# Two-layer transformer trunk on one core: the hidden product of both MLPs with weight blocks as stationary operand and 256 tokens as moving one

## What is computed

```python
def sq_relu_mlp(h, w1, w2):          # w1: (2048, 8192), w2: (8192, 2048)
    return jnp.square(jax.nn.relu(h @ w1)) @ w2

h = modulate(rms_norm(x, norm_g[layer, 1]), shift_m, scale_m)
x = x + gate_m[:, None, :] * sq_relu_mlp(h, mlp_w1[layer], mlp_w2[layer])
```

## Time and profile before

| | |
|---|---|
| runs of the kernel before, median of 3 | 2586.66 us (2586.28 to 2590.52) |
| profiled execution, its own time | 2587.83 us |
| its span in the trace | 2586.0 us |
| granted TensorE clock, mean over the span | 0.979 |
| first MLP with its entry, about 690 to 1495 us of the span | 805 us |
| second MLP with its entry, about 1840 us to the end | 746 us |
| weights and `ada` matrices read from HBM | 661 MB, 257 GB/s over the span |

### The profile page before, as it was taken

One profiled execution on the slowest core, in us unless ns is written; L12 is line 12 of the kernel. 1 busy time (PEld: TensorE's weight loads), 2 busy tenths in 40 slices (PEclk: granted clock), 3 DMA queues, 4 the chain that ended last, 5 costly groups with the idle time before them and its releaser, 6 DMA issues.

```text
span 2586.0 us, 27843 instructions
## 1 busy us (share of the span) xinstructions
PE 2403.0 (93%) x10901; PEld 1970.1 (76%) x10901; DVE 1848.6 (71%) x2145; ACT 1185.4 (46%) x1931; POOL 72.9 (3%) x128
## 2 busy tenths in 40 slices
PE   0299999997999999999998989999899999999999
PEld 0288888876787888888887877777687888888887
DVE  7778786877788677677776767877796555555554
ACT  1256556564543443443445664554543443443442
POOL 1100000000100000000001010000100000000000
PEclk9599999999999999999999999999999999999999
DMA  8688696866788777777785867856696555555554
GB/s 358 270 296 306 220 342 233 328 252 236 292 302 308 261 282 275 276 289 267 280 301 207 316 230 282 312 210 254 263 368 211 189 187 187 187 186 188 187 187 163
DMA packets 150466, 665.23 MB, mean 257 GB/s; under 512 B 16864, under 2 KB 17344, under 8 KB 120896
## 3 DMA queue, kind: packets, MB, share of 16 engines
q1 hardware_dynamic: 150336, 663.46, 70.3%
HBM read 661.30 MB, written 2.10 MB: 257 GB/s over the span
## 4 chain that ended last, share of the span: by engine, by line
PE 75%; DVE 12%; ACT 5%; DMA 4%; issue 4%; POOL 0%; SPq 0%; DVEq 0%; ACTq 0%
PE main L359 24%; PE main L361 24%; PE main L360 24%; DVE acc L916 5%; DVE w_lo L899 3%; DMA w_raw<-w 2%; PE tr L372 2%; ACT w_hi L644 1%; DMA ada_raw<-ada 1%; ACT st_a L684 1%; PE tr L414 1%; DMA qT<-ada 1%; ACT sm L717 1%; PE tr L435 0%; ACT st_b L670 0%
## 5 line engine op out<-in xcount | busy, mean ns | idle before, releaser
L644 ACT ACTIVATE w_hi<-w_raw 128x1024 fp32r<-128x1024 f32 x800 | 844.1, 1060 | 1105.0 <-DMA w_raw<-w 1104.6
L899 DVE TENSOR_TENSOR w_lo<-w_raw,w_hi 128x1024 fp32r<-128x1024 f32 x800 | 971.6, 1222 | 438.4 <-ACT w_hi L644 434.9
L359 PE MATMUL main<-w_hi,hT_hi 128*128 128x512 f32 x2176 | 869.4, 400 | 7.0 <-DVE w_lo L899 2.9
L361 PE MATMUL main<-w_hi,hT_lo 128*128 128x512 f32 x2176 | 851.5, 391 | 0.0
L360 PE MATMUL main<-w_lo,hT_hi 128*128 128x512 f32 x2176 | 850.8, 391 | 0.0
L916 DVE SCALAR_TENSOR_TENSOR acc<-ada_raw,c_act,acc 128x2048 f32<-128x2048 f32 x194 | 455.7, 2349 | 50.2 <-DMA ada_raw<-ada 47.8
L359 PEld LDWEIGHTS main<-w_hi,hT_hi 128*128 128x128 f32 x2176 | 411.6, 189 | 93.4 <-DVE w_lo L899 5.2
L361 PEld LDWEIGHTS main<-w_hi,hT_lo 128*128 128x128 f32 x2176 | 410.5, 189 | 86.9
L360 PEld LDWEIGHTS main<-w_lo,hT_hi 128*128 128x128 f32 x2176 | 411.3, 189 | 83.4 <-issue 1.2
L359 PE MATMUL main<-w_hi,mid_hi 128*128 128x512 f32 x1024 | 406.1, 397 | 0.0
L361 PE MATMUL main<-w_hi,mid_lo 128*128 128x512 f32 x1024 | 404.0, 395 | 0.0
(11 more groups left out here) (155 smaller groups left out, 1166.7 us busy)
## 6 DMA issues: line engine op xcount, KB each, us to landing
w_raw<-w SPq DMA_DIRECT2D x800, 512.0 KB, 3.4
ada_raw<-ada SPq DMA_DIRECT2D x208, 1024.0 KB, 6.5
qT<-ada SPq DMA_DIRECT2D x16, 1024.0 KB, 7.2
gate<-bias_rows SPq DMA_DIRECT2D x4, 1024.0 KB, 6.5
xs<-x SPq DMA_DIRECT2D x1, 2048.0 KB, 9.2
out<-xs SPq DMA_DIRECT2D x4, 512.0 KB, 5.3
st_a<-lamb SPq DMA_DIRECT2D x1, 256.0 KB, 4.7
gain_rot_sb<-gain_rot SPq DMA_DIRECT2D x1, 160.0 KB, 2.9
```

The lines of the kernel that those rows point to most:

```text
L359: pe.matmul(acc_ps[:, :], hi[:, kt, tc], w_hi[:, s, wc], start=(kt == 0), stop=False)
L361: last = pe.matmul(acc_ps[:, :], lo[:, kt, tc], w_hi[:, s, wc], start=False, stop=(kt == PK * pairs - 1))
L644: act.activation(w_hi[:, s, :], w_raw[:, s, :], ACT.Copy).then_inc(hi_done, 1)
L899: dve.tensor_tensor(w_lo[:, s, :], w_raw[:, s, :], w_hi[:, s, :].bitcast(F32), ALU.subtract).then_inc(lo_done, 1)
```

## The change

Only the first product of the MLPs changes, and what stands between it and the second. A new function `hidden_gemm` takes the place of `gemm` for the 16 first-product chunks of each MLP. The stationary operand is now a 128x128 block of the weights, the moving one all 256 tokens of `hT`. A piece is 24 matmuls of 256 columns in place of 12 of 512, a chunk 192 in place of 96. The result has hidden columns on partitions and tokens along the free dimension, two blocks of 128 hidden columns in each bank. Relu and square work on it as before, only in another layout; `mid_hi` and `mid_lo` are then made from `st_b` directly, at place 6 in place of 7. The transposes, their waits for `tr` and the semaphore `mid_full` are gone. The second product waits by a new semaphore, `mid_split`, and a semaphore `squared` orders the square before its readers. On VectorE the release of the bank now stands behind a wait for its own two squares.

```diff
+            def hidden_gemm(par, side=None, ready=None):
+                claim_main(par)
+                for j in range(PIECES):
...
+                    pe.wait_ge(lo_done, n["w"].n)
+                    for k in range(PK):
+                        kt = PK * j + k
+                        for f in range(NC // P):
+                            wc, odd = slice(k * NC + f * P, k * NC + (f + 1) * P), f % 2
+                            acc_ps = main[par][f // 2][:, odd * T * P:(odd + 1) * T * P]
+                            pe.matmul(acc_ps, w_hi[:, s, wc], hT_hi[:, kt, :], start=(kt == 0 and odd == 0), stop=False)
+                            pe.matmul(acc_ps, w_hi[:, s, wc], hT_lo[:, kt, :], start=False, stop=False)
+                            last = pe.matmul(acc_ps, w_lo[:, s, wc], hT_hi[:, kt, :], start=False,
+                                             stop=(kt == KT - 1 and odd == 1))
...
             def mlp(sums, gate_at):
                 side, ready = build()
-                gemm(0, *h, side=side, ready=ready)
+                hidden_gemm(0, side=side, ready=ready)
...
-                    def hidden(par):
-                        def step():
-                            pe.wait_ge(read_out[par], n[f"ro{par}"].n + 1)
-                            for kp in range(2):
-                                claim_tr(kp)
-                                pair_transposes(
-                                    kp, lambda k, t: stb[:, t, (PK * kp + k) * P:(PK * kp + k + 1) * P]
-                                ).then_inc(mid_full, 1)
...
-                        pe.wait_ge(tr_free[j % 2], first[j % 2] + j // 2 + 2 + late)
+                        pe.wait_ge(mid_split, made + j + 1)
...
-                    sides = [{2: [hidden(1 - c % 2)]} for c in range(1, 5)] + [{}, {}, {}]
+                    sides = [{} for c in range(7)]
...
-                                act.wait_ge(mid_full, n["mid"].up())
-                                kt = 4 * c + PK * kp
-                                act.activation(mid_hi[:, kt:kt + PK, :],
-                                               tr[kp][:, :].rearrange("p (k n) -> p k n", k=PK),
+                                act.wait_ge(squared, n["squared"].up())
+                                kt = 4 * c + PK * b
+                                act.activation(mid_hi[:, kt:kt + PK, :].rearrange("p k n -> p (k n)"), stb[:, b, :],
...
-                        last.then_inc(read_out[par], 1)
+                            last.then_inc(squared, 1)
+                        dve.wait_ge(squared, n["squared"].up(2))
+                        dve.sem_inc(read_out[par], 1)
...
-                    sides = [{4: [square(1 - c % 2)], 7: [mid(c - 1)]} for c in range(1, 5)]
+                    sides = [{4: [square(1 - c % 2)], 6: [mid(c - 1)]} for c in range(1, 5)]
```

More of the change, by code:

```diff
@@ L221, in trunk @@
         vec_full, col_full, row_full = sem("vec_full"), sem("col_full"), sem("row_full")
-        hT_full, mid_full, qk_full, pt_full = sem("hT_full"), sem("mid_full"), sem("qk_full"), sem("pt_full")
+        hT_full, qk_full, pt_full = sem("hT_full"), sem("qk_full"), sem("pt_full")
         modulated = sem("modulated")
@@ L230, in trunk @@
         x_rms, x_rstd, x_done = sem("x_rms"), sem("x_rstd"), sem("x_done")
-        relu_done = sem("relu_done")
+        relu_done, squared, mid_split = sem("relu_done"), sem("squared"), sem("mid_split")
         smx_done, p_done, mix_done = sem("smx_done"), sem("p_done"), sem("mix_done")
@@ L362, in gemm @@
                                              stop=(kt == PK * pairs - 1))
+                    last.then_inc(mm_done, 1)
+                    for step in (side or {}).get(j, ()):
+                        step()
+            def hidden_gemm(par, side=None, ready=None):
+                claim_main(par)
+                for j in range(PIECES):
+                    n["w"].up()
+                    s = (n["w"].n - 1) % SLOTS
+                    if ready:
+                        ready(j)
+                    pe.wait_ge(lo_done, n["w"].n)
[8 more added lines that the diff above has]
+                                             stop=(kt == KT - 1 and odd == 1))
                     last.then_inc(mm_done, 1)
@@ L560, in mlp @@
                 side, ready = build()
-                gemm(0, *h, side=side, ready=ready)
+                hidden_gemm(0, side=side, ready=ready)
                 def block(number, last=False):
-                    first = [n["tr0"].n, n["tr1"].n]
-                    def hidden(par):
-                        def step():
-                            pe.wait_ge(read_out[par], n[f"ro{par}"].n + 1)
-                            for kp in range(2):
-                                claim_tr(kp)
-                                pair_transposes(
-                                    kp, lambda k, t: stb[:, t, (PK * kp + k) * P:(PK * kp + k + 1) * P]
-                                ).then_inc(mid_full, 1)
-                        return step
+                    made = n["mid"].n
+                    n["mid"].up(PIECES)
                     def mid_ready(j):
-                        late = 2 if number == 0 and j >= 2 * (gate_at + 1) else 0
-                        pe.wait_ge(tr_free[j % 2], first[j % 2] + j // 2 + 2 + late)
-                    sides = [{2: [hidden(1 - c % 2)]} for c in range(1, 5)] + [{}, {}, {}]
+                        pe.wait_ge(mid_split, made + j + 1)
+                    sides = [{} for c in range(7)]
                     if number == 0:
-                        sides[gate_at] = also(sides[gate_at], halves(sum_rows, 5))
+                        sides[gate_at] = halves(sum_rows, 5)
                     if sums:
@@ L587, in block @@
                     for c in range(1, 4):
-                        gemm(c % 2, *h, side=sides[c - 1])
+                        hidden_gemm(c % 2, side=sides[c - 1])
                     for c in range(4):
@@ L591, in block @@
                     if not last:
-                        gemm(0, *h)
+                        hidden_gemm(0)
                 block(0)
@@ L840, in step @@
                         def step():
-                            for kp in range(2):
-                                act.wait_ge(mid_full, n["mid"].up())
-                                kt = 4 * c + PK * kp
-                                act.activation(mid_hi[:, kt:kt + PK, :],
-                                               tr[kp][:, :].rearrange("p (k n) -> p k n", k=PK),
+                            for b in range(2):
+                                act.wait_ge(squared, n["squared"].up())
+                                kt = 4 * c + PK * b
+                                act.activation(mid_hi[:, kt:kt + PK, :].rearrange("p k n -> p (k n)"), stb[:, b, :],
                                                ACT.Copy).then_inc(hi_part, 1)
@@ L849, in block @@
                     for c in range(1, 4):
-                        chunk(PIECES, {4: [relu(1 - c % 2)], 7: [mid(c - 1)]})
-                    chunk(PIECES, {4: [relu(1)], 7: [mid(3)]})
+                        chunk(PIECES, {4: [relu(1 - c % 2)], 6: [mid(c - 1)]})
+                    chunk(PIECES, {4: [relu(1)], 6: [mid(3)]})
                     for c in range(1, 4):
@@ L1265, in step @@
                     def step():
-                        for kp in range(2):
-                            dve.wait_ge(mid_full, n["mid"].up())
+                        for b in range(2):
                             dve.wait_ge(hi_part, n["hi"].up())
[L1269 to L1273, removed]
+                            kt = 4 * c + PK * b
+                            dve.tensor_tensor(mid_lo[:, kt:kt + PK, :].rearrange("p k n -> p (k n)"), stb[:, b, :],
+                                              mid_hi[:, kt:kt + PK, :].rearrange("p k n -> p (k n)").bitcast(F32),
+                                              ALU.subtract).then_inc(mid_split, 1)
                     return step
                 def block(i, last=False):
-                    sides = [{4: [square(1 - c % 2)], 7: [mid(c - 1)]} for c in range(1, 5)]
+                    sides = [{4: [square(1 - c % 2)], 6: [mid(c - 1)]} for c in range(1, 5)]
                     sides += [{4: [update(c)]} for c in range(3)]
```

## The result

The changed kernel takes 2597.97 us (median of 7 runs, 2594.41 to 2599.28) against 2587.22 for the kernel before (7 runs, 2586.28 to 2590.52): **10.8 us slower**, ratio 1.0042, 95% interval 1.0032 to 1.0052. The forecast was 2566. The size is that of rival 3, 2600 us. The profiled execution took 2596.75 us, 8.9 more than the one of before.

What follows compares the result with a forecast made beforehand. The prediction took TensorE's serial work to bound the kernel. Transposes -28.3, width +5 and give-back +2 made -21 us off the median 2586.7, so 2566 us; range 2550 to 2612, the forecast's own 2553 to 2577.

Steps and rivals of the forecast that it cites:

- rival 3: First-product matmuls: 13.4 ns lost per matmul, 120.1 ns each, +41 us, so 2600 us; against the change from 118 ns; chance 0.20.
- What bounds the kernel: Whole kernel: TensorE's serial work sets the time; in an MLP an instruction removed or lengthened there counts in full.
- The transposes, -28.3 us: Both MLPs: 256 transposes between first and second product, 0.110 us each, all on the path, are removed.
- The width, +5 us: First product: 3072 matmuls of 512 columns become 6144 of 256 at 114.2 ns; each pair takes 1.7 ns more.
- the value that I take: a share of the stream: First-product matmuls: most of the 13.4 ns loss halves with the columns, 1.7 ns stays fixed, giving 114.2 ns per matmul.
- Rival 1: First product: load-bound and quicker, narrow matmuls at 112 ns like the f32 passes, 2553 us; chance 0.11.
- Rival 2: First product: even, a fixed share of 9 ns, 117.9 ns per matmul, +28 us, so 2587 us; chance 0.14.
- Rival 4: First product: load and stream share their reads, 136 ns per matmul, +139 us, so 2698 us; chance 0.08.
- Rival 5: MLPs: become bound by VectorE or transfers elsewhere, most of the 21 us turns into waits, about 2584 us; chance 0.05.
- The give-back, +2 us: First block of first MLP: three first-product chunks' gains of 0.7 us each are lost in TensorE's wait for VectorE's sums.
- a wait whose end does not move: First block of first MLP: TensorE arrives sooner, but its 1.37 us wait for VectorE's sums ends at the same time.
- fixed share of 64 ns: Each matmul, by a straight line through the skill's 81 and 131 ns: 197 us on 3072 more matmuls; the forecast rejected it.

Runs made afterwards that it cites:

- the width alone: Kernel before with each 512-column first-product matmul issued as two of 256, tokens still stationary, transposes kept: 2625.56 us, ratio 1.0158.

## Why the prediction was wrong

- **What bounds the kernel**: right. What was removed and what was added on TensorE counted in full, within the intervals.
- **The transposes, -28.3 us**: right; 26 to 27 us when removed alone. The two rows of the kernel before that the 1.11 us were read from:

```profile
2452.65 1.04 PE L372 MATMUL tr<-ident,st_b 128*128 128x128 f32 x8
...
2453.76 0.40 PE L360 MATMUL main<-w_lo,hT_hi 128*128 128x512 f32 x1
```

- **The width, +5 us**: wrong, and the step that failed is "the value that I take: a share of the stream". That term put 225 of the 226.7 ns down to the stream, to halve with the columns, and left 1.7 as fixed; 13.3 are fixed. A matmul of 256 columns takes 120.0 ns, not 114.2; a pair 240.0, 13.3 more than one of 512, and 3072 of these are +41 us, as the width alone showed. Both reasons given for the choice were true rows wrongly read. That nothing is lost at the lower clock does not exclude a fixed loss, since the changed kernel has one of 13.3 ns at the higher clock and none at the lower. That a load beside the stream costs nothing excludes only that the load slows the stream, and the run with half the stationary operand, which got no quicker, fits that; a loss between two matmuls is left possible by it. The price of rival 3, 120.1 ns and +41 us, was the right one, from the same row.
- **Rival 1** (112 ns) is the floor that 128 columns show and 256 do not reach. **Rival 2** (117.9) took its fixed share from f32 passes, of which the shorter was at that floor. **Rival 4** is out: 136 ns are far from 120.0, and half the load did not help. **Rival 5** is out: PE's idle time did not grow.
- The argument for rival 3, that the second product loses 19.1 ns with the same moving operand, did not support it: 5.7 of these come from where `mid` lies. Its condition was right and this ground for it was not.
- **The give-back, +2 us**: wrong, though small. What failed is "a wait whose end does not move": in the run without the transposes and with 512 columns TensorE came over 5 us sooner and did not wait at all. The 1.37 us were those of one trace.
- The sum with the measured price, -28.3 + 41, is +12.7; measured +10.8 (8.3 to 13.4).

The Trainium skill's isolated gap (TensorE: Matmul & The Clock Gate, "Back-to-back issue gap") is the columns' time plus 2.5 ns at 2.4 GHz, and the columns' time alone at 1.2 GHz. By it, an estimate, a pair of 256 would cost 2.5 ns more than one of 512. The traces agree with its form, a fixed addition at the higher clock and none at the lower, which is the form that the forecast ruled out; they do not agree with its size, since these fp32r matmuls have 13.3 ns. The 81 and 131 ns that the same section gives for a stream, and the fixed share of 64 ns estimated from them in the prediction, agree with no run here: 226.7 ns at 512 columns, and a fixed 13.3.

What stays open: what the 13.3 ns are, and whether each matmul pays them or each change of the stationary operand, since every matmul here has a load of its own (a kernel with bf16 operands was not run, nor one without loads); why half a stationary operand costs 3.3 ns more; and what in the distance makes the other loss, for which the table has no simple law.

## What to carry to other kernels

Price a narrower matmul by matmuls, not by columns: the same sums in twice as many instructions cost the fixed part twice, here 13.3 ns x 3072, more than 256 transposes of 0.110 us. When a fixed part and a share of the stream explain the same row, the present trace can't choose; half width in the old orientation would have told in one run. And look at the steps of like matmuls in different stages: a difference of 2.5% between two products with the same moving tile was a matter of 128 bytes of padding, worth 17 us, more than the change itself.

## What the runs showed of the hardware that was not expected

- fp32r matmuls, each with its own load, lose 13.3 ns each at the higher clock (226.7 ns for 512 columns, 120.0 for 256, about 175 for 384), whichever operand holds the weights; at the lower clock none (427 and 213.8 ns). With 128 columns they take 112 ns.
- The step depends on the distance of the two operands in SBUF modulo 256 bytes, between 226.6 and 234.3 ns for 512 columns; moves of 8 or 16 bytes change it by up to 7 ns.
- A stationary operand of 64 columns is slower than one of 128: 230.0 against 226.7 ns.
- The quickest version with all its sums is the kernel before with 128 bytes of padding ahead of `mid_hi`: 2570.35 us, ratio 0.9935.
